# Splitting the first block's projections and summing the experts by token rows in a two-block fp32 model kernel

## The chip, the cores and the metric

The kernel runs on one core of a Trainium2 chip. Its engines are TensorE (PE: matmuls, and PEld: its weight loads), VectorE (DVE), ScalarE (ACT), GpSimd (POOL) and SyncE (SP, which only issues DMAs here). Each runs its own instruction list in order and waits on semaphores. The metric is the device time of one execution, in microseconds (us).

## The reference, cut to what matters

256 tokens of 1024 features (plus 16 meta tokens in the first block) go through two transformer blocks, all in float32:

```python
# first block
proj = rmsnorm(h) @ w_in                 # sb_q, sb_k, sb_v, df_q, df_k, df_v: 1024 columns each
o_sb = stick_breaking(sb_q, sb_k, sb_v)  # 8 heads
o_df = diff_attn(df_q, df_k, df_v)       # 8 heads
gates = sigmoid(xn @ w_gate + b_gate)    # 2048 columns
h = h + (gates[0] * (o_sb @ w_br_sb) + gates[1] * (o_df @ w_br_df)) @ w_out
h = h + (silu(hn @ w_ffn_gate) * (hn @ w_ffn_up)) @ w_ffn_down
x = rmsnorm(h)
# second block
mod = silu(c) @ w_ada + b_ada            # 6 x 1024: shifts, scales, gains gt_a and gt_f
...                                      # retention, dilated attention, projections
x = x + gt_f * moe(modulated norm of x)  # 32 experts, top 4 of each token
return rms_norm(x, g_final)
```

An expert takes the tokens routed to it through `u = x @ w1 + b1`, a clamped SwiGLU and `a @ w2 + b2`, and its result is added to the tokens' rows with their gate weights.

## The kernel before, in words

**Projections of the first block.** Activations lie feature by feature (`xn`: 8 tiles k of 128 features x 272 tokens). The weights come in 20 pieces of 1024 x 512 (`PIECES1`): sq, sk, sv twice, dq, dk, dv twice, four of gate, and two each of ysb, ydf and out. A piece makes four groups; the list of groups is `GR1`, and `G` steps in `ORDER1` are its groups. For the first 16 pieces a q, k or gate group is 8 plain float32 products of 256 or 272 columns (`group`, L1619), which the trace shows as two matmul records each. A v piece is a small group for the meta rows (L1602), two groups of 8 products with 512 columns, and one product that adds the meta rows up (L1608). The last six pieces are split: ScalarE rounds a quarter of a piece (128 x 1024 elements) to a high part (`high1`), VectorE subtracts it to get the low part (`low1`), and TensorE makes three products (high x high, high x low, low x high) in the fp32r type instead of one (`three`, L1629 to L1631). `high1` and `low1` run three groups ahead of the products.

**The attention heads lie between the groups.** `order1` gives every step a position: `G` g stands at position g, and a chain (start, period, heads, steps) puts step s of head h at start + period x h + offset. At one position head steps come before the group, later heads first. All engines walk through this one order, each doing its share of a step and skipping steps in which it has none. For the eight sb heads: `sbA` makes the scores (PE, L1672 to L1674), scales them (ACT), clips them (DVE), takes exp and ln (ACT) and finishes with three DVE operations, the last of them L1134; `sbB` multiplies by a triangle (PE, L1680 to L1685) and goes through DVE and ACT; `sbC` multiplies by the values (PE, L1694 to L1696). For the df heads there are `dfA` to `dfD`.

**Modulation.** The product with `w_ada` is made on VectorE: `modulation(j)` sums eight weighted rows of a 1024 x 512 piece of `w_ada` (L1088, then L1091 and L1093: eight operations, j = 0 to 11) into `adac`, and TensorE adds up the partitions in `ada_mm(j)` (L1663), which waits for that sum (`ada_sum`). `ada_mm` stands at the head of TensorE's part of `sbC` (j = h), and of `dfC` for the first four df heads (j = 8 + h).

**Experts.** Before them the router picks experts (DVE) and TensorE turns the tokens to rows (`htok`, L1932). For each expert TensorE gathers 64 tokens (L1986), makes `u` in four pieces (`up1`, L1976), `y` (L2013) and scatters the result back by `scatter` (L1960), which VectorE adds to `acc`. `acc` lies feature by feature; it starts as the bias term (L2033, eight products, copied by DVE at L1509) between expert 0 and expert 1. SP loads 12.6 MB of weights for an expert into six ring slots; piece c of the next expert's `w1` is loaded when `up1` has used that slot. After the last expert DVE adds `acc` times the gain to the residual (L1553), a norm follows (squares on ACT, L1564 on PE, root on ACT, L1048 on DVE), TensorE turns the result to token rows (L1932), ACT copies it, and one DMA stores 1 MB.

## Time and profile before

| | |
|---|---|
| median of 3 runs | 1971.28 us (1970.89 to 1972.0) |
| the profiled execution's own time | 1971.77 us |
| its span, first to last instruction | 1970.0 us |
| mean granted TensorE clock | 0.977 of 2.4 GHz |
| busy: PE, PEld | 1863.7 us, 1239.0 us |
| busy: DVE, ACT, POOL | 711.1 us, 554.3 us, 27.2 us |
| moved by DMA | 568.57 MB |

The profile is of one execution. Its span is 1.8 us less than its own time. "Busy" of PE counts overlapping matmuls, so it does not say at what rate they run; the spacing of starts does. PEclk is the granted clock, 1.00 for 2.4 GHz and 0.50 for 1.2 GHz.

### The profile page before, as it was taken

What the parts mean: (1) busy time and instruction counts of PE and PEld (TensorE: products, weight loads), DVE (VectorE), ACT (ScalarE), POOL (GpSimd) and SP (SyncE); (2) the same over time, 40 slices, a digit from 0 to 9 for tenths busy, and PEclk for the clock granted to TensorE, in tenths of its full rate; (3) what the DMA queues carried; (4) which work ended last, traced back from release to release, by engine and by line L of the source; (5) the groups of instructions that cost most, each with busy time, mean ns of one, the idle gap of its engine ahead of it and who ended that gap; (6) DMA issues with size and microseconds to landing.
All of it is one profiled execution on the core that took longest, in us unless ns stands there. A gap on an engine that the chain in (4) does not pass through costs nothing.

```text
span 1970.0 us, 26848 instructions
## 1 busy us (share of the span) xinstructions
PE 1863.7 (95%) x10951; PEld 1239.0 (63%) x10952; DVE 711.1 (36%) x1269; ACT 554.3 (28%) x916; POOL 27.2 (1%) x49
## 2 busy tenths in 40 slices
PE   7999989989998999999989999999999999999996
PEld 6666757989998799889853444344344344344343
DVE  2345533656654644546431222122122122122113
ACT  2344346544344455555410101001001000010002
POOL 2000000000000000000000000000000000000000
PEclk9999999999999999999879999999999999999997
DMA  7666423546554654534849999999999999999992
GB/s 245 221 215 214 171 86 129 171 134 195 184 206 135 201 179 150 170 109 166 315 177 378 428 430 428 429 428 429 428 429 428 429 428 429 428 429 428 429 428 111
DMA packets 135055, 568.57 MB, mean 289 GB/s; under 512 B 5552, under 2 KB 77336, under 8 KB 110288
## 3 DMA queue, kind: packets, MB, share of 16 engines
q1 hardware_dynamic: 127056, 536.60, 68.6%
q0 software_dynamic: 7936, 31.07, 4.5%
q8 instruction: 47, 0.77, 0.2%
q14 instruction: 16, 0.13, 0.0%
HBM read 566.58 MB, written 3.43 MB: 289 GB/s over the span
## 4 chain that ended last, share of the span: by engine, by line
PE 61%; DMA 33%; ACT 3%; DVE 2%; issue 1%; SPq 0%; DVEq 0%
DMA s_ring<-in_w_mlp 32%; PE banks L1619 11%; PE banks L1976 10%; PE banks L1629 6%; PE banks L1631 6%; PE banks L1630 6%; PE banks L1758 3%; PE banks L1759 3%; PE banks L1760 3%; PE banks L2013 3%; PE banks L1986 2%; PE banks L1564 1%; PE banks L1960 1%; PE banks L1663 1%; DVE s_W L1048 1%
## 5 line engine op out<-in xcount | busy, mean ns | idle before, releaser
L1976 PE MATMUL banks<-s_ring,s_W 128*64 128x512 f32 x2048 | 461.9, 599 | 29.1 <-DMA s_ring<-in_w_mlp 29.0
L1976 PEld LDWEIGHTS banks<-s_ring,s_W 128*64 128x64 f32 x2048 | 139.6, 137 | 319.1 <-issue 257.4
L1465 DVE TENSOR_TENSOR s_W<-banks,s_W 128x512 f32<-128x512 f32 x128 | 82.1, 683 | 633.7 <-PE banks L1960 633.7
L2013 PE MATMUL banks<-s_ring,s_W 128*64 128x512 f32 x1024 | 227.3, 597 | 0.3 <-ACT s_W L1000 0.3
L1619 PE MATMUL banks<-s_W,s_ring 128*128 128x256 f32 (+1 forms) x768 | 180.0, 391 | 4.6 <-DVE s_W L1048 4.6
L1619 PEld LDWEIGHTS banks<-s_W,s_ring 128*128 128x128 f32 x768 | 146.1, 193 | 33.6 <-issue 10.5
L2013 PEld LDWEIGHTS banks<-s_ring,s_W 128*64 128x64 f32 x1024 | 73.7, 138 | 148.2 <-issue 133.7
L1264 DVE TENSOR_TENSOR r_w2l<-s_ring,r_w2h 128x1024 fp32r<-128x1024 f32 x96 | 116.9, 1223 | 83.9 <-ACT r_w2h L865 83.7
L1005 ACT ACTIVATE s_W<-banks 128x512 f32<-128x512 f32 x32 | 19.1, 597 | 431.0 <-PE banks L2013 431.0
L1629 PE MATMUL banks<-r_x2h,r_w2h 128*128 128x256 f32 x448 | 130.7, 292 | 6.1 <-DVE r_x2l L1278 6.1
L1986 PEld LDWEIGHTS banks<-s_W 128*128 128x128 f32 x1024 | 123.2, 200 | 13.5 <-issue 11.4
L1986 PE MATMUL banks<-s_W 128*128 128x64 f32 x1024 | 127.7, 286 | 2.7 <-DVE s_W L1509 1.7
L1631 PE MATMUL banks<-r_x2h,r_w2l 128*128 128x256 f32 x448 | 127.4, 284 | 0.0
L1630 PE MATMUL banks<-r_x2l,r_w2h 128*128 128x256 f32 x448 | 127.3, 284 | 0.0
L865 ACT ACTIVATE r_w2h<-s_ring 128x1024 fp32r<-128x1024 f32 x96 | 100.8, 1053 | 46.2 <-PE banks L1631 36.3
L1009 ACT ACTIVATE s_W<-s_W 128x512 f32<-128x512 f32 x32 | 20.2, 631 | 325.4 <-DVE s_W L1483 325.4
L1758 PE MATMUL banks<-r_xfh,r_wh 128*128 128x256 f32 x352 | 100.4, 285 | 6.7 <-DVEq L1249 6.7
L1217 DVE TENSOR_TENSOR r_wl<-s_ring,r_wh 128x1024 fp32r<-128x1024 f32 x66 | 80.5, 1223 | 63.0 <-ACT r_wh L816 62.5
L1759 PE MATMUL banks<-r_xfl,r_wh 128*128 128x256 f32 x352 | 100.2, 285 | 0.0
L1760 PE MATMUL banks<-r_xfh,r_wl 128*128 128x256 f32 x352 | 100.1, 284 | 0.0
L1629 PEld LDWEIGHTS banks<-r_x2h,r_w2h 128*128 128x128 f32 x448 | 86.6, 193 | 7.6 <-issue 7.3
L1630 PEld LDWEIGHTS banks<-r_x2l,r_w2h 128*128 128x128 f32 x448 | 86.6, 193 | 0.5 <-issue 0.2
(382 smaller groups left out, 2770.0 us busy)
## 6 DMA issues: line engine op xcount, KB each, us to landing
s_ring<-in_w_mlp SPq DMA_DIRECT2D x192, 2048.0 KB, 22.4
s_ring<-in_w_in SPq DMA_DIRECT2D x38, 1024.0 KB, 5.0
s_ring<-in_w_in SPq DMA_DIRECT2D x12, 2048.0 KB, 9.1
...
```

Of the source, the lines that this page charges most:

```text
L865: act.activation(w2h[:, n % 4, :].rearrange("p (k n) -> p k n", k=raw.shape[1]), raw, ACT.Copy).then_inc(S["w_hi"], 1)
L1264: tt(unit2(w2l, n), raw, w2h[:, n % 4, :].bitcast(F32).rearrange("p (k n) -> p k n", k=raw.shape[1]), ALU.subtract).then_inc(S["w_lo"], 1)
L1619: last = mm(o, lhs, rhs, start=k == 0, stop=k == nk - 1)
L1629: mm(out, a[0], b[0], start=start, stop=False)
L1630: mm(out, a[0], b[1], start=False, stop=False)
L1631: return mm(out, a[1], b[0], start=False, stop=stop)
L1758: mm(out, wh[:, i, v], xh, start=start, stop=False, skip_group_check=True)
L1759: mm(out, wh[:, i, v], xl, start=False, stop=False, skip_group_check=True)
L1760: return mm(out, wl[:, i, v], xh, start=False, stop=stop, skip_group_check=True)
L1976: last = mm(pb[b][64 * h:64 * h + 64, :], XgT[:, 2 * c + k, :], slot(c, 2)[:, k, 1024 * h + 512 * b:1024 * h + 512 * b + 512], start=False ...
L1986: last = mm(pb[3][:, 64 * k:64 * k + 64], htok[:, t, P * k:P * k + P], selU[:, t, :], start=t == 0, stop=t == 1)
L2013: last = mm(pb[2][64 * h:64 * h + 64, :], aT[:, k, 64 * c:64 * c + 64], slot(4 + c, 4)[:, k, 512 * h:512 * h + 512], start=c == 0 and k == ...
```

## The change

Four things are changed.

1. The first 16 pieces are split like the last six. `xn` gets a high and a low part (`xnh`, `xnl`), and every q, k and gate group becomes 24 fp32r products. A v piece becomes four units of 18 products with 512 columns, over three row tiles (16 meta rows, 128 and 128 tokens), without the separate adding of meta rows. Positions of `ORDER1` are now units (`UNITS1`); pieces still have four. Weights come in halves of 1 MB throughout.
2. The heads start at unit 9 instead of group 12. `sbC` stands at offset 4 (was 3), `dfB` at 2.9 (2), `dfC` at 4 (3), `dfD` at 5 (4).
3. A modulation's eight operations are eight steps, `ada0` to `ada7`, three eighths of a unit apart, from unit 10 (it was one step at group 11, 14, ...).
4. `acc` lies by token rows and starts as residual plus bias term: TensorE makes rows of the gain (`spread`), turns the residual (`hx`) by products with the unit matrix, and adds the scaled bias term before expert 0. `yv` is multiplied by the gain on VectorE instead of copied on ScalarE. `scatter` has two products of 512 columns instead of four of 256. The final norm works by rows: two squares with a sum on ACT, two roots, two DVE operations, and a store for each half.

The gate and up products of the first block's feed-forward part are not touched.

```diff
-PIECES1 = ([(side + kind, n, i) for side in "sd" for i in range(2) for kind, n in (("q", 4), ("k", 4), ("v", 4))]
+PIECES1 = ([(side + kind, n, i) for side in "sd" for i in range(2) for kind, n in (("q", 4), ("k", 4), ("v", 3))]
...
 def order1():
-    return weave(len(GR1), (SB_AT, 3, HEADS, {"sbA": 0, "sbB": 2, "sbC": 3}),
-                 (SB_AT - 1, 3, ADAS, {"ada": 0}),
-                 (SB_AT + 3 * HEADS + 1, 3, HEADS, {"dfA": 0, "dfB": 2, "dfC": 3, "dfD": 4}),
...
+    return weave(len(UNITS1), (SB_AT, 3, HEADS, {"sbA": 0, "sbB": 2, "sbC": 4}),
+                 (SB_AT + 1, 3, ADAS, {f"ada{k}": 3 * k / KT for k in range(KT)}),
+                 (SB_AT + 3 * HEADS + 1, 3, HEADS, {"dfA": 0, "dfB": 2.9, "dfC": 4, "dfD": 5}),
...
-SB_AT = 12
+SB_AT = 9
...
         act.activation(vec[:, 0:NVEC], pb[5][:, 0:NVEC], ACT.Copy).then_inc(S["vec_kept"], 1)
+        for n in range(2):
+            high1(n)
         act.wait_ge(S["filled"], 1)
         root(0, rms, TM)
+        for t in range(KT):
+            act.wait_ge(S["norm_x"], t + 1)
+            act.activation(xnh[:, t, :], xn[:, t, :], ACT.Copy).then_inc(S["xn_hi"], 1)
+        high1(2)
...
+        for t in range(KT):
+            dve.wait_ge(S["xn_hi"], t + 1)
+            tt(xnl[:, t, :], xn[:, t, :], xnh[:, t, :].bitcast(F32), ALU.subtract).then_inc(S["xn_lo"], 1)
...
+            if k == 0:
+                if j >= 2:
+                    dve.wait_ge(S["ada_mm"], j - 1)
+                dve.wait_ge(S["csil"], 1)
+                dve.wait_ge(ina[b], 16 * (j // 2 + 1))
+                last = ts(adac[:, b, :], w[:, 0, :], csil[:, 0:1], None, ALU.mult)
+            else:
+                dve.wait_ge(S["ada_sum"], KT * j + k)
+                last = stt(adac[:, b, :], w[:, k, :], csil[:, k:k + 1], adac[:, b, :], ALU.mult, ALU.add)
+            last.then_inc(S["ada_sum"], 1)
...
         def ada_mm(j):
-            pe.wait_ge(S["ada_sum"], j + 1)
+            pe.wait_ge(S["ada_sum"], KT * (j + 1))
...
+        def spread(bank, cols, n):
+
+            for j in range(4):
+                c = cols[:, 4 * n + j:4 * n + j + 1].broadcast_to([P, P])
+                last = mm(pb[bank][:, P * j:P * j + P], c, ident, start=True, stop=True)
+            return last
...
-        for t in range(KT):
-            stt(hx[:, t, :], acc[:, t, :], modT[:, 40 + t:41 + t], hx[:, t, :], ALU.mult, ALU.add).then_inc(S["final_sum"], 1)
-        norm(5, hn, hx, nrms, vrows("g_final"))
+        dve.sem_inc(S["final_sum"], 1)
+        dve.wait_ge(S["spread_kept"], 6)
+        for t in range(2):
+            dve.wait_ge(S["fin_sq"], t + 1)
+            st.do(nc.vector.reciprocal(tr[:, t:t + 1], tr[:, t:t + 1]))
+            st.wait()
+            stt(otok[:, t, :], acc[:, t, :], tr[:, t:t + 1], gfb, ALU.mult, ALU.mult).then_inc(S["fin_kept"], 1)
```

What order each engine's instructions stand in, at three places. First VectorE, before: the eight operations of modulation 0 (L1088, L1091, L1093), then `sbA` of head 0 (L1127 to L1134).

```order
L1088 TENSOR_SCALAR s_W<-s_W,s_vx 128x512 [waits ada_in0,csil,cst_in]
L1091 SCALAR_TENSOR_TENSOR s_W<-s_W,s_vx 128x512 [waits dve_step] x6
L1093 SCALAR_TENSOR_TENSOR s_W<-s_W,s_vx 128x512 [waits dve_step]
L1127 TENSOR_SCALAR s_ring<-s_ring 128x384 [waits sb_zs]
L1128 TENSOR_SCALAR s_ring<-s_ring 16x256
L1131 TENSOR_TENSOR s_ring<-s_ring 128x384 [waits sb_ln]
L1132 TENSOR_TENSOR s_ring<-s_ring 16x256
L1134 TENSOR_TENSOR s_ring<-s_ring,s_cst 128x2x128 [waits dve_step]
```

VectorE now, at the `sbA` step of head 1 (L1157 to L1164): three steps of modulation 0 (L1122), the `sbA` step, the low part of a weight unit (L1084), the last two steps of modulation 0, and the first step of modulation 1 (L1119).

```order
L1122 SCALAR_TENSOR_TENSOR s_W<-s_W,s_vx 128x512 [waits ada_sum] x3
L1157 TENSOR_SCALAR s_ring<-s_ring 128x384 [waits sb_ln,sb_zs]
L1158 TENSOR_SCALAR s_ring<-s_ring 16x256
L1161 TENSOR_TENSOR s_ring<-s_ring 128x384 [waits sb_ln]
L1162 TENSOR_TENSOR s_ring<-s_ring 16x256
L1164 TENSOR_TENSOR s_ring<-s_ring,s_cst 128x2x128 [waits dve_step]
L1084 TENSOR_TENSOR r_w2l<-s_ring,r_w2h 128x8x128 [waits w1_hi]
L1122 SCALAR_TENSOR_TENSOR s_W<-s_W,s_vx 128x512 [waits ada_sum] x2
L1119 TENSOR_SCALAR s_W<-s_ring,s_vx 128x512 [waits ada_in1,csil]
```

Modulation 0 stood wholly ahead of `sbA` of head 0; now its last two steps stand behind `sbA` of head 1 and a weight unit. Modulations 1 to 6 stand likewise behind `sbA` of heads 2 to 7.

Second TensorE, before: `sbA` of head 1 (L1672 to L1674), `ada_mm(0)` (L1663) and `sbC` of head 0 (L1694 on), and the next group (L1619).

```order
L1672 MATMUL banks<-s_W 128x256 [waits sb_zs,act_evac1]
L1673 MATMUL banks<-s_W 128x128
L1674 MATMUL banks<-s_W 16x256
L1663 MATMUL banks<-s_ones,s_W 128x1 [waits ada_sum,act_evac1,sb_a]
L1663 MATMUL banks<-s_ones,s_W 128x1 x3
L1694 MATMUL banks<-s_ring,s_W 128x256
L1619 MATMUL banks<-s_W,s_ring 128x256 [waits act_evac1]
```

TensorE now, from `sbA` of head 1 (L1679 to L1681): unit 12 (24 products, L1626 to L1628), then `ada_mm(0)` (L1670) and `sbC` of head 0 (L1701), then the next unit.

```order
L1679 MATMUL banks<-s_W 128x256 [waits sb_zs,act_evac1]
L1680 MATMUL banks<-s_W 128x128
L1681 MATMUL banks<-s_W 16x256
L1626 MATMUL banks<-r_xnh,r_w2h 128x256 [waits act_evac1,w1_lo]
L1627 MATMUL banks<-r_xnl,r_w2h 128x256
L1628 MATMUL banks<-r_xnh,r_w2l 128x256
...
L1670 MATMUL banks<-s_ones,s_W 128x1 [waits ada_sum,act_evac1,sb_a]
L1670 MATMUL banks<-s_ones,s_W 128x1 x3
L1701 MATMUL banks<-s_ring,s_W 128x256
L1626 MATMUL banks<-r_xnh,r_w2h 128x256 [waits act_evac1,w1_lo]
```

One unit now stands between `sbA` of head h + 1 and `sbC` of head h, and `ada_mm` still waits for the modulation's last step.

Third TensorE ahead of the experts, before: tokens turned to rows (L1932), the router's ranks (L1943 on), the gate weights turned (L1949), gather of expert 0 (L1986), bias rows (L1967), `up1` (L1976), then the bias term (L2033) and the gather of expert 1 (rows that only repeat are left out).

```order
L1932 MATMUL banks<-s_cst,s_W 128x128 x16
L1943 MATMUL banks<-s_W,s_cst 128x32 [waits route]
L1949 MATMUL banks<-s_cst,s_W 32x128 x2
L1986 MATMUL banks<-s_W 128x64 [waits selu,rank_done,ht_kept]
L1967 MATMUL banks<-r_b1r,r_selB 128x512 [waits selb]
L1976 MATMUL banks<-s_ring,s_W 64x512 [waits expert_in0,xg]
L2033 MATMUL banks<-s_W 128x256 [waits gt_kept]
L1986 MATMUL banks<-s_W 128x64 [waits xg,selu,acc_init]
```

TensorE now: two `spread` of the gain (L1954), the residual turned (L1962), ranks (L1965), gate weights turned (L1972), the bias term (L1978), gather of expert 0 (L2012), `up1` (L2002), two `spread` of the final gain (L1954) and the gather of expert 1.

```order
L1939 MATMUL banks<-s_cst,s_W 128x128 x16
L1954 MATMUL banks<-s_cst,s_modT 128x128 x8
L1962 MATMUL banks<-s_cst,s_hT 128x128 [waits ht_kept]
L1965 MATMUL banks<-s_W,s_cst 128x32 [waits route]
L1972 MATMUL banks<-s_cst,s_W 32x128 [waits spread_kept]
L1978 MATMUL banks<-s_W 128x512 [waits b2_scaled,gt_kept]
L2012 MATMUL banks<-s_W 128x64 [waits selu,rank_done]
L1993 MATMUL banks<-r_b1r,r_selB 128x512 [waits selb]
L2002 MATMUL banks<-s_ring,s_W 64x512 [waits expert_in0,xg]
L1954 MATMUL banks<-s_cst,s_vec 128x128 [waits acc_init]
L2012 MATMUL banks<-s_W 128x64 [waits xg,selu]
```

The bias term has moved from behind expert 0 to ahead of its gather, and waits there for VectorE's scaled bias (`b2_scaled`).

## Rows read from the trace of the kernel before

**Rows 1.** the page's chain that ended last, by line, share of the span

```profile
DMA s_ring<-in_w_mlp 32%; PE banks L1619 11%; PE banks L1976 10%; PE banks L1629 6%; PE banks L1631 6%; PE banks L1630 6%; PE banks L1758 3%; PE banks L1759 3%; PE banks L1760 3%; PE banks L2013 3%; PE banks L1986 2%; PE banks L1564 1%; PE banks L1960 1%; PE banks L1663 1%; DVE s_W L1048 1%
```

**Rows 2.** stages: busy time by engine, granted clock, DMA share, GB/s

```profile
245.00:300.00 55.00, 50.01 (x217) 32.49 (x216) 19.68 (x50) 23.87 (x57) 0.00 (x0) 0.97 0.26 92
...
1200.00:1930.00 730.00, 700.11 (x3766) 307.78 (x3764) 151.95 (x320) 64.47 (x125) 0.00 (x0) 1.00 1.01 429
```

**Rows 3.** timeline and two lines' listings (ns min/median/max, first and last start), projections

```profile
53.17 1.92 PE L1602 MATMUL banks<-s_ring,s_W 128*32 128x512 f32 x16
69.92 0.48 PE L1672 MATMUL banks<-s_W 128*128 128x256 f32 x1
...
237.53 3.83 PE L1619 MATMUL banks<-s_W,s_ring 128*128 128x272 f32 x16
...
346.46 7.07 PE L1619 MATMUL banks<-s_W,s_ring 128*128 128x256 f32 x32
...
677.93 0.40 PE L1630 MATMUL banks<-r_w2l,r_x2h 128*128 128x512 f32 x1
...
689.53 0.39 PE L1630 MATMUL banks<-r_w2l,r_x2h 128*128 128x512 f32 x1
...
L1631 PE MATMUL banks<-r_dfh,r_w2l x64: 283/283/283, 376.6 to 399.3; 128*128 128x256 f32 x64
...
L1619 PE MATMUL banks<-s_W,s_ring x768: 379/379/634, 22.8 to 353.2; 128*128 128x256 f32 x128, 128*128 128x272 f32 x64
```

**Rows 4.** timeline and a window at the start of the projections

```profile
22.19 3.39 DVE L1048 SCALAR_TENSOR_TENSOR s_W<-s_hT,s_vec,s_ring 128x272 f32<-128x272 f32 x8 [8.10 <-ACT s_ring L678]
22.84 30.41 PE L1619 MATMUL banks<-s_W,s_ring 128*128 128x256 f32 x128 [4.64 <-DVE s_W L1048]
...
24.00:26.00 2.00, 2.00 (x6) 1.64 (x5) 1.97 (x6) 0.00 (x0) 0.00 (x0) 0.50 0.00 0
```

**Rows 5.** timeline around one sbA step (head 2): scores, chain, modulation

```profile
101.77 0.60 PE L1674 MATMUL banks<-s_W 128*16 128x256 f32 x2
102.30 1.05 PE L1663 MATMUL banks<-s_ones,s_W 128*128 128x1 f32 x8
...
107.87 0.42 DVE L1134 TENSOR_TENSOR s_ring<-s_ring,s_cst 128x256 f32<-128x256 f32 x1
...
108.73 4.69 DVE L1091 SCALAR_TENSOR_TENSOR s_W<-s_ring,s_vx,s_W 128x512 f32<-128x512 f32 x6
```

**Rows 6.** the page's groups: the split's two passes in the second block, mean ns

```profile
L1264 DVE TENSOR_TENSOR r_w2l<-s_ring,r_w2h 128x1024 fp32r<-128x1024 f32 x96 | 116.9, 1223 | 83.9 <-ACT r_w2h L865 83.7
...
L865 ACT ACTIVATE r_w2h<-s_ring 128x1024 fp32r<-128x1024 f32 x96 | 100.8, 1053 | 46.2 <-PE banks L1631 36.3
```

**Rows 7.** timeline: TensorE after a wait in the second kind of heads

```profile
274.82 0.30 PE L1719 MATMUL banks<-s_cst,s_ring 128*128 128x128 f32 x1 [2.90 <-ACT s_ring L762]
...
275.40 5.31 PE L1619 MATMUL banks<-s_W,s_ring 128*128 128x256 f32 x16
```

**Rows 8.** timeline and a window from routing to the second expert

```profile
995.07 7.06 PE L1986 MATMUL banks<-s_W 128*128 128x64 f32 x32 [0.99 <-DVE s_W L1452]
...
1003.02 15.70 PE L1976 MATMUL banks<-s_ring,s_W 128*64 128x512 f32 x64
1018.65 3.72 PE L2033 MATMUL banks<-s_W 32*128 32x256 f32 x16
...
1024.10 7.09 PE L1986 MATMUL banks<-s_W 128*128 128x64 f32 x32 [1.73 <-DVE s_W L1509]
...
1036.00:1038.00 2.00, 2.00 (x12) 0.67 (x10) 0.00 (x0) 0.00 (x0) 0.00 (x0) 1.00 0.00 0
...
1084.45 3.79 PE L1986 MATMUL banks<-s_W 128*128 128x64 f32 x32
```

**Rows 9.** timeline at the end of the program

```profile
1950.64 3.25 DVE L1553 SCALAR_TENSOR_TENSOR s_hT<-s_W,s_modT,s_hT 128x256 f32<-128x256 f32 x8 [1.58 <-issue]
...
1965.66 0.40 SPq L611 DMA_DIRECT2D out<-s_W  x1
```

More of the change, by code:

```diff
@@ L363, in program @@
     htok = area(W, 2048, 2, D)
[L364 removed]
+    acc = area(W, 4096, 2, D)
     selU = area(W, 6144, 2, 64)
@@ L985, in _ @@
                            ACT.Copy).then_inc(S["ht_kept"], 1)
+        for b in range(2):
+            act.wait_ge(S["spread"], b + 1)
+            act.activation(gtb[:, 512 * b:512 * b + 512], pb[3 - b], ACT.Copy).then_inc(S["spread_kept"], 1)
         act.wait_ge(S["route"], 1)
@@ L1011, in _ @@
         expert(0, True, False)
+        for b in range(2):
+            act.wait_ge(S["spread"], b + 3)
+            act.activation(gfb[:, 512 * b:512 * b + 512], pb[6 + b], ACT.Copy).then_inc(S["spread_kept"], 1)
         expert(1, True, True)
@@ new lines, in first_unit @@
+            if kind in V_KINDS:
+                groups = UNITS1[n // 4 * 4 + 3]
+                for kk in range(2):
+                    k = 2 * (n % 4) + kk
+                    for i, g in enumerate(groups):
+                        if k == 0:
+                            bank_free(GR1, g, both)
+                        v, rows = (slice(0, M), M) if i == 0 else (slice(M + P * (i - 1), M + P * i), P)
+                        last = three(pb[g % 3][0:rows, :], (xnh[:, k, v], xnl[:, k, v]), (whi[:, kk, :], wlo[:, kk, :]), k == 0, k == KT - 1)
+                        if k == KT - 1:
+                            last.then_inc(S["gemm1"], 1)
+                if n % 4 < 3:
+                    last.then_inc(S["v_unit1"], 1)
+                return
@@ new lines, in first_unit @@
+            xh, xl = {"ydf": (dfh, dfl), "ysb": (yh, yl), "out": (yh, yl)}.get(kind, (xnh, xnl))
+            tokens = slice(M, TM) if kind in ("sq", "dq", "gate") else slice(0, xh.shape[2])
+            for g in UNITS1[n]:
+                bank_free(GR1, g, both)
+                for k in range(KT):
+                    if n == 0:
+                        pe.wait_ge(S["xn_lo"], k + 1)
+                    if kind == "out":
+                        pe.wait_ge(S["y_lo"], 4 + k + 1)
+                    x = (xh[:, k, tokens], xl[:, k, tokens])
+                    last = three(pb[g % 3][:, 0:x[0].shape[1]], (whi[:, k, :], wlo[:, k, :]), x, k == 0, k == KT - 1)
+                last.then_inc(S["gemm1"], 1)
```

342 lines of the change are left out of this document (151 added, 191 removed).

## The prediction

> **What bounds the kernel now.** I read the page's chain first. Its largest link is the stream of expert weights (32% of the span), and most of the rest is TensorE, with L1619, the first block's products, at 11% [rows 1]. The windows agree: between 1200 and 1930 us the DMA engines are busy all the time (share 1.01, 429 GB/s), while in the first block, 245 to 300 us, TensorE works 50.0 of 55 us at DMA share 0.26 [rows 2]. So an instruction saved on TensorE, ACT or DVE per expert is worth nothing after 1200 us; what counts is the first block, the entry to the experts until the stream is the bound, and the tail. I read those at the spacing of starts, since busy time counts overlaps. The sum is made against the profiled execution's 1971.8 us (span 1970.0 and 1.8 around it), 0.5 above the median.
>
> **Projections on TensorE.** 32 records of 256 columns took 7.07 us; without the last record's 0.38, 31 spacings of 0.216 are left, so a q or gate group costs 3.45 us. A k group (272 columns, 3.83 for 16) costs 16 x 0.230 = 3.68. A v piece took from 53.17 to 69.92, 16.75 [rows 3]. The split products: 63 spacings from 376.6 to 399.3 us make one triple 0.360, so 24 products cost 2.88. With 272 columns the nearest row is that one times 272/256, 3.06 (bounds 2.88 and 3.45). For 512 columns, 677.93 to 689.53 is 17 triples, 0.227 a product, so the 72 products of a v piece cost 16.4 [rows 3]. Sum: 32 x 0.57 = -18.2, 16 x 0.62 = -9.9, 4 x 0.35 = -1.4: **-29.5**. The two passes for a weight unit, 1.05 us on ACT and 1.22 on DVE [rows 6], are shorter than a unit and lie beside it, so alone they add nothing.
>
> The Trainium skill ("FP8 and Floating Point Precision", TensorE Precision Notes) says that a true float32 product takes four passes; three passes for four would bring a group of 3.45 to 2.59 and this term to -42. The rows give 17% off, not 25%; I go by them.
>
> **Start.** Today the first product starts at 22.84, behind the first of eight multiplications that last 3.39 us together, and TensorE is at 0.50 of its clock then [rows 4]. Now two `high1` (2 x 1.05 [rows 6]) stand ahead of ACT's root, and then all eight low parts (about 0.45 each) stand on DVE behind all eight multiplications. First complete product: 22.84 + 2.1 + 3.4 less what overlaps, about 28. **+4.9** (bounds +2, the two passes alone, and +7, if the first two units' low parts hold the multiplications up as well).
>
> **A new wait at `sbC`.** This is the term that decides. `ada_mm(h)` opens TensorE's part of `sbC(h)` and waits for the eighth operation of modulation h. The order shows its last two operations behind `sbA(h + 1)` and one low part on VectorE; on TensorE a single unit lies between the same `sbA(h + 1)` and `ada_mm(h)`. Today the chain of an `sbA` runs on ACT and DVE in turn: scores end at 102.37, L1134 ends at 108.29, 5.9 us later, in which DVE is held by waits for ACT [rows 5]. Behind it come the low part 1.22 [rows 6], two operations of 0.78 [rows 5] and some 0.2 of signalling: ready 8.9 us after the scores. TensorE arrives after one unit, 2.9 (a v unit 4.1). Wait 6.0 for six heads and 4.8 for the one with a v unit, h = 0 to 6: **+40.8**. Queued behind the waiting `ada_mm` are `sbC(h)` and all later units; nothing overtakes. Head 7 has no `sbA` behind it and the df heads' `ada_mm` stands after `dfA`, whose DVE part is shorter. Lower bound of a wait: where TensorE arrives a unit later, 8.9 - 5.8 = 3.1; upper bound: 8.9, if it arrives at once.
>
> **The clock after such a wait.** At 274.82 TensorE had stood 2.90 us, and the next 16 records took 5.31 us where half of 7.07 is usual: +1.8. The opening groups show the same level, 0.50 at 24 to 26 us [rows 3, 4, 7]. Seven waits twice as long: 7 x 1.8 = **+12.6** (0, if a wait has no such price, to +18 with a longer slow stretch).
>
> The Trainium skill ("TensorE: Matmul & The Clock Gate", Part 1, on the clock gate) says that an idle TensorE falls back to half its clock and oscillates when gaps repeat; by this rule the 12.6 stands, and the trace's one row of 5.31 us agrees.
>
> **df heads and gates.** Today TensorE stands 5 of 55 us there and DVE works 19.7, which is 1.5 and 5.8 in a head of 16 us [rows 2]. On DVE a head now gains three low parts, 3.7 [rows 6], and the first four heads still have a modulation's eight operations, 6.2 [rows 5]: 15.7, about what TensorE needs, 16 - 1.5 - 3 x 0.57 = 12.8 and its waits. So up to 8 x 1.7 of the projections' saving can be lost to waits for DVE and ACT here; against that stand the wider steps of `dfB` to `dfD`. I take **+4** (0, all waits as before, to +8).
>
> Block 1: -29.5 + 4.9 + 40.8 + 12.6 + 4 = **+32.8**; the first block's other parts stay, so its first `ysb` product, behind the groups that end today at 346.46 + 7.07 [rows 3], starts near 386 instead of 353.
>
> **Entry to the experts.** The bias term costs 3.72 us now, and its copies 1.73 of waiting before the next gather, which also runs at half clock, 7.09 where the later one at 1084 us takes 3.79 [rows 8]. All of it leaves from behind expert 0: -5.45 and -3.3. In its place there comes the final gain's `spread`, half the columns: +1.9. Ahead of gather 0 come the bias term's products, as many columns as before (3.7, at half clock near 7), and ACT's copies and DVE's scaling of 1024 columns, 1.2 each; TensorE had been waiting 0.99 there for routing anyway, so part lies beside it. I take +4 (2 to 9). Net **-3** (-6.5 to +2). All of this counts in full, since the stream of weights stands still at 1036 us (DMA share 0.00) until `up1` of expert 1 frees a slot [rows 8]. In the steady part `scatter`, `yv` and their waits lie under the stream (share 1.01 [rows 2]): 0, and if that cover went, DVE's multiplication for ACT's copy would cost a few tenths of a us per expert.
>
> **Tail.** From L1553 at 1950.64 to the span's end is 19.4 us, 4.3 of it behind the store's issue at 1965.66 [rows 9]. In its place: two squares of 1024 columns on ACT (1.05 each by [rows 6]), a root and a reciprocal (0.2 each, my estimate from these rows' small operations), one multiplication of 1024 columns on DVE (1.5 by twice 0.78 [rows 5]) and a store of half the size (4): 8.1. **-11** (-9 to -12).
>
> **Sum:** 32.8 - 3 - 11 = +18.8, so 1990.6 against the profiled execution and **1990** against the median.
>
> **Rivals.**
> (a) *Faster: the modulation is done in time.* If DVE runs ahead of TensorE, so that the last two operations are ready when `ada_mm` comes up, the 40.8 and 12.6 vanish: 1971.3 - 29.5 + 4.9 + 4 - 3 - 11 = 1937 us. For that L1134's successor would have to end within half a microsecond of the scores; today's 5.9 speaks against it. The sign turns at a price per head (wait and clock) of (53.4 - 18.8) / 7 = 4.9 us, where I have 7.6. Chance 0.10, reaching to 1967.
> (b) *The waits come, but the clock does not fall:* 12.6 less, 1977 us. For it: the price rests on one row [rows 7]; against it: the waits are twice as long as the one there. Chance 0.14, from 1968 to 1982.
> (c) *DVE bounds all the df heads, and the entry stays at half clock:* +4 for the first, and +6 for the second (gather and bias term slow): 2000 us. For it: DVE's 15.7 a head; against: only four heads have modulations. Chance 0.17.
> (d) The sum as it stands, 1982 to 1996: chance 0.59.
>
> A measurement of this kernel tells about 0.2%, 4 us, from no change. Slower by more are (d), (c) and half of (b): 0.83. Within it 0.06, faster 0.11, from (b) and (a). The range leaves out (a) and the far end of (c): 1971 to 2003.
>
> **What the profile after would show.** TensorE idle some 6 us before `ada_mm` (L1670), released by DVE's L1122, seven times between 75 and 215 us, and a granted clock below 1 there; q units at 2.9 us; the first `ysb` product near 386 us; DMA share 1.0 between 1200 and 1930 still; some 8 us from the last addition to `acc` to the end. I am wrong if the waits at L1670 are under 4 us or bring no slow clock, if the last operation of an `sbA` (L1164 now) ends well before 5.9 us after its scores, or if the split products with 272 or 512 columns cost more than those of 256 per column.

## The result, and the profile after

The changed kernel takes 2018.99 us (median of 4 runs, 2016.09 to 2023.51); the kernel before, timed beside it, 1971.64 (1970.89 to 1972.42). The ratio is 1.0242, with a 95% interval of 1.022 to 1.0264: 47 us slower, where 19 were forecast (range up to 2003). The sign was right and the size was not. The profiled execution is the fastest of the four, with a span of 2014.5 us, 44.5 more than before.

The page's chain that ended last, by engine and by line, in the changed kernel:

```profile
PE 54%; DMA 33%; DVE 7%; ACT 5%; issue 2%; SPq 0%; DVEq 0%; ACTq 0%
DMA s_ring<-in_w_mlp 32%; PE banks L2002 9%; PE banks L1626 8%; PE banks L1628 7%; PE banks L1627 7%; PE banks L1765 3%; PE banks L1766 3%; PE banks L1767 3%; PE banks L2039 2%; DVE s_W L1122 2%; DVE r_w2l L1084 2%; PE banks L2012 1%; PE banks L1593 1%; ACT r_w2h L699 1%; PE banks L1670 1%
```

The stream of expert weights is still 32% of it [rows 1], but VectorE lines that were not there now are: L1122, a modulation step, and L1084, the low part of a weight unit. The list of waits (engine and line that waited, who released it, us in total, times, longest) names one for TensorE:

```profile
PE banks L1670 <- DVE s_W L1122: 45.7, 8, 7.2
```

These are eight waits of `ada_mm`, 45.7 us, the last of them 0.98 us; the seven before it make 44.7. One of them in full, around `sbA` of head 1 (timeline: start us, us, operation, idle before and its releaser):

```profile
75.95 0.61 PE L1681 MATMUL banks<-s_W 128*16 128x256 f32 x2
...
82.41 0.42 DVE L1164 TENSOR_TENSOR s_ring<-s_ring,s_cst 128x256 f32<-128x256 f32 x1
82.75 1.22 DVE L1084 TENSOR_TENSOR r_w2l<-s_ring,r_w2h 128x1024 fp32r<-128x1024 f32 x1
83.89 1.53 DVE L1122 SCALAR_TENSOR_TENSOR s_W<-s_W,s_vx 128x512 f32<-128x512 f32 x2
...
85.57 1.84 PE L1670 MATMUL banks<-s_ones,s_W 128*128 128x1 f32 x8 [5.98 <-DVE s_W L1122]
```

This is [rows 5] with the new things behind it: the scores end at 76.56, the chain 82.83, the low part and the last two modulation steps follow without a gap, and TensorE, after its single unit, has stood 5.98 us. The next row is what was not foreseen in its size. The windows of the same stretch (us, busy time of PE, PEld, DVE, ACT, POOL, granted clock, DMA share, GB/s), and after them those of the kernel before around its wait of 2.90 us [rows 7]:

```profile
79.00:82.00 3.00, 0.59 (x6) 0.39 (x4) 0.50 (x2) 2.97 (x5) 0.00 (x0) 1.00 0.27 94
82.00:83.50 1.50, 0.00 (x0) 0.00 (x0) 1.47 (x4) 0.67 (x2) 0.00 (x0) 0.57 0.00 0
85.00:95.00 10.00, 9.43 (x37) 8.40 (x38) 3.46 (x5) 1.33 (x2) 0.88 (x1) 0.50 0.60 210
95.00:97.00 2.00, 2.00 (x11) 1.46 (x9) 0.00 (x0) 1.48 (x2) 0.00 (x0) 0.78 0.19 25
```

```profile
275.00:276.00 1.00, 1.00 (x8) 0.91 (x7) 0.20 (x1) 0.56 (x3) 0.00 (x0) 1.00 1.04 406
276.00:279.00 3.00, 3.00 (x9) 2.36 (x9) 0.00 (x0) 0.34 (x2) 0.00 (x0) 0.52 1.04 395
279.00:280.00 1.00, 1.00 (x5) 0.86 (x4) 0.00 (x0) 0.00 (x0) 0.00 (x0) 0.73 0.08 27
280.00:282.00 2.00, 2.00 (x16) 1.28 (x15) 0.35 (x1) 0.48 (x1) 0.00 (x0) 1.00 0.00 0
```

The clock (1.00 is 2.4 GHz, 0.50 is 1.2) fell while TensorE idled and stayed at 0.50 through all of 85 to 95 us. Before, it fell after the wait had ended and was down for about 3.5 us. So `ada_mm`, `sbC` and most or all of a unit run at half speed in each of the seven heads (granted clock 0.50 to 0.59 from `ada_mm` to the next `sbB`), not only part of one group.

The kernel before has another row that bears on this. Behind its wait of 1.73 us ahead of the gather of expert 1 [rows 8] the clock was down for some 10 us, although the wait was shorter:

```profile
1022.00:1024.00 2.00, 0.37 (x2) 0.00 (x0) 2.00 (x4) 0.00 (x0) 0.00 (x0) 0.91 1.05 451
1024.00:1026.00 2.00, 1.91 (x9) 1.91 (x10) 0.64 (x3) 0.00 (x0) 0.00 (x0) 0.50 1.00 426
1032.00:1034.00 2.00, 2.00 (x7) 0.89 (x7) 0.00 (x0) 0.87 (x2) 0.00 (x0) 0.53 0.00 0
```

Ten microseconds at half speed are a price of about 5 us. Three other waits of that trace, 1.43, 1.81 and 2.05 us in the heads, cost nothing: the clock stayed at 1.00 behind them.

The stages one by one. The first product comes at 28.03 instead of 22.84 [rows 4]. The first block ends 57.3 us later (the first product behind its norm at 490.77, before at 433.50). The router's first product is at 1032.54, before at 974.99: the stretch between is the same within 0.3 us. From there to the third expert (the last row is cut off by the end of the view):

```profile
1055.33 7.19 PE L1978 MATMUL banks<-s_W 32*128 32x512 f32 x8 [0.46 <-ACT s_W L999]
1062.45 7.09 PE L2012 MATMUL banks<-s_W 128*128 128x64 f32 x32
1070.43 1.12 PE L2002 MATMUL banks<-s_ring,s_W 128*64 128x512 f32 x2
...
1087.00 3.68 PE L2012 MATMUL banks<-s_W 128*128 128x64 f32 x32
...
1114.77 1.44 PE L2012 MATMUL banks<-s_W 128*128 128x64 f32 x11
```

Gather 0 starts 29.9 us behind the router's first product (before 20.1 [rows 8]). Of these 9.8 us, 7.1 are the bias products, which ran at half clock, and 3.2 come before them: the ranks start 20.0 us behind the router's first product instead of 16.8, since VectorE now scales the bias rows first (1.21 us) and waits for ScalarE's copy of the gain until 1046.37. Behind gather 0 the time comes back: the gather of expert 1 takes 3.68 instead of 7.09, and from gather 0 to the third gather there are 52.3 us instead of 61.5. Up to the third gather the kernel is 0.7 us behind. The tail is 7.7 us from the first square to the span's end, and was 19.4 [rows 9]:

```profile
2006.77 1.06 ACT L1050 ACTIVATE s_W<-s_W 128x1024 f32<-128x1024 f32 x1 [12.65 <-DVEq L1577]
...
2009.86 1.74 SPq L616 DMA_DIRECT2D out<-s_W  x2
2009.94 1.28 DVE L1583 SCALAR_TENSOR_TENSOR s_W<-s_W,s_sml 128x1024 f32<-128x1024 f32 x1
```

Sum: 57.3 for the first block less 11.7 for the tail leaves 45.6 of the span's 44.5, so everything between gave back 1.1 and not 3. That is not from the entry either: what gave time back lies behind the third gather, 2.1 us, 1.1 of it in the last expert's `y` products, which took 8.10 us instead of 9.22 with less of them at half clock.

### The profile page after: what moved, and what is told of

It is laid out like the page before. It is cut to its first block, busy times and chain, and to the rows that moved or that the text cites. A ratio compares the mean times of both kernels' runs of the same rounds, so it can differ in the third digit from the quotient of the medians.

```text
span 2014.5 us, 27568 instructions
## 1 busy us (share of the span) xinstructions
PE 1858.4 (92%) x11191; PEld 1248.1 (62%) x11192; DVE 803.1 (40%) x1358; ACT 594.1 (29%) x952; POOL 27.1 (1%) x49
## 4 chain that ended last, share of the span: by engine, by line
PE 54%; DMA 33%; DVE 7%; ACT 5%; issue 2%; SPq 0%; DVEq 0%; ACTq 0%
DMA s_ring<-in_w_mlp 32%; PE banks L2002 9%; PE banks L1626 8%; PE banks L1628 7%; PE banks L1627 7%; PE banks L1765 3%; PE banks L1766 3%; PE banks L1767 3%; PE banks L2039 2%; DVE s_W L1122 2%; DVE r_w2l L1084 2%; PE banks L2012 1%; PE banks L1593 1%; ACT r_w2h L699 1%; PE banks L1670 1%
## 5 line engine op out<-in xcount | busy, mean ns | idle before, releaser
L2002 PE MATMUL banks<-s_ring,s_W 128*64 128x512 f32 x2048 | 460.6, 597 | 29.1 <-DMA s_ring<-in_w_mlp 29.1
L2002 PEld LDWEIGHTS banks<-s_ring,s_W 128*64 128x64 f32 x2048 | 139.1, 137 | 331.1 <-issue 258.6
L1501 DVE TENSOR_TENSOR s_W<-banks,s_W 128x512 f32<-128x512 f32 x32 | 22.1, 692 | 461.1 <-PE banks L2039 461.1
L1285 DVE TENSOR_TENSOR r_w2l<-s_ring,r_w2h 128x1024 fp32r<-128x1024 f32 x96 | 116.9, 1223 | 85.3 <-ACT r_w2h L872 85.0
L1084 DVE TENSOR_TENSOR r_w2l<-s_ring,r_w2h 128x1024 fp32r<-128x1024 f32 x88 | 107.3, 1223 | 91.2 <-ACT r_w2h L699 90.7
L1488 DVE TENSOR_TENSOR s_W<-banks,s_W 128x512 f32<-128x512 f32 x128 | 82.2, 684 | 147.5 <-PE banks L1987 147.5
L1626 PE MATMUL banks<-r_x2h,r_w2h 128*128 128x256 f32 x448 | 131.2, 293 | 6.1 <-DVE r_x2l L1299 6.1
L2012 PEld LDWEIGHTS banks<-s_W 128*128 128x128 f32 x1024 | 120.0, 196 | 24.2 <-issue 24.2
L1626 PE MATMUL banks<-r_xnh,r_w2h 128*128 128x256 f32 (+1 forms) x384 | 120.1, 313 | 9.7 <-DVE r_xnl L1092 9.7
L1628 PE MATMUL banks<-r_x2h,r_w2l 128*128 128x256 f32 x448 | 127.8, 285 | 0.0
L2012 PE MATMUL banks<-s_W 128*128 128x64 f32 x1024 | 124.3, 281 | 0.0
L1627 PE MATMUL banks<-r_xnl,r_w2h 128*128 128x256 f32 (+1 forms) x384 | 114.9, 299 | 0.0
L1628 PE MATMUL banks<-r_xnh,r_w2l 128*128 128x256 f32 (+1 forms) x384 | 114.8, 299 | 0.0
L872 ACT ACTIVATE r_w2h<-s_ring 128x1024 fp32r<-128x1024 f32 x96 | 100.8, 1053 | 46.1 <-PE banks L1628 39.7
L699 ACT ACTIVATE r_w2h<-s_ring 128x1024 fp32r<-128x1024 f32 x88 | 92.0, 1049 | 33.8 <-PE banks L1628 29.3
## 6 DMA issues: line engine op xcount, KB each, us to landing
s_ring<-in_w_mlp SPq DMA_DIRECT2D x192, 2048.0 KB, 22.4
```

What stands on the lines that cost most here:

```text
L699: act.activation(w2h[:, n % 4, :].rearrange("p (k n) -> p k n", k=raw.shape[1]), raw, ACT.Copy).then_inc(S["w1_hi"], 1)
L872: act.activation(w2h[:, n % 4, :].rearrange("p (k n) -> p k n", k=raw.shape[1]), raw, ACT.Copy).then_inc(S["w_hi"], 1)
L1084: tt(unit1(w2l, n), raw, w2h[:, n % 4, :].bitcast(F32).rearrange("p (k n) -> p k n", k=raw.shape[1]), ALU.subtract).then_inc(S["w1_lo"], 1)
L1285: tt(unit2(w2l, n), raw, w2h[:, n % 4, :].bitcast(F32).rearrange("p (k n) -> p k n", k=raw.shape[1]), ALU.subtract).then_inc(S["w_lo"], 1)
L1626: mm(out, a[0], b[0], start=start, stop=False)
L1627: mm(out, a[0], b[1], start=False, stop=False)
```

## The experiments

The theory, A: the modulation's last two operations stand on VectorE behind the next `sbA`, TensorE waits for them seven times, and each wait also costs the clock, some 4 us each and not 1.8. The price was worked out before the runs by adding the seven stretches from `ada_mm` to the next `sbB` (67.8 us in the changed kernel) against their length at full clock. The rivals: VectorE is simply overloaded; the clock is not the idling's doing; it is the new schedule as a whole that loses, so that the split under the old offsets would gain. The first four ran on one chip, the next four on another, the last four on a third; each ratio is against the kernel before on the same chip.

| run | base | median us | ratio (95%) |
|---|---|---|---|
| e_early | changed kernel | 1953.83 | 0.9911 (0.9894 to 0.9927) |
| e_whole | changed kernel | 1959.46 | 0.9940 (0.9924 to 0.9957) |
| e_fill | changed kernel | 1993.83 | 1.0115 (1.0098 to 1.0132) |
| e_sched | changed kernel | 1966.26 | 0.9984 (0.9974 to 0.9994) |
| e_half | kernel before | 1959.68 | 0.9942 (0.9928 to 0.9955) |
| e_start | e_early | 1948.70 | 0.9876 (0.9861 to 0.9891) |
| e_moe | e_early | 1953.31 | 0.9904 (0.9889 to 0.9920) |
| e_all | e_early | 1950.81 | 0.9892 (0.9877 to 0.9907) |
| e_c5 | changed kernel | 1994.23 | 1.0110 (1.0091 to 1.0130) |
| e_ada2 | e_start | 1949.40 | 0.9891 (0.9875 to 0.9906) |
| e_warm | e_start | 1946.95 | 0.9867 (0.9852 to 0.9882) |
| e_best | e_start | 1941.48 | 0.9855 (0.9839 to 0.9871) |

**e_early: one number.**

```diff
-                 (SB_AT + 1, 3, ADAS, {f"ada{k}": 3 * k / KT for k in range(KT)}),
+                 (SB_AT, 3, ADAS, {f"ada{k}": 3 * k / KT for k in range(KT)}),
```

> The changed kernel with one number altered: the eight modulation steps start one unit earlier, so that the last two stand ahead of sbA(h + 1) on VectorE and not behind it. Theory A (the wait at ada_mm is made by that place): the seven waits, 44.7 us together, and the half clock after them, some 28.6 us worked out from the changed kernel's trace, vanish: 2019 - 73 = 1946 us, between 1942 and 1956 with new small waits. Rival B (VectorE is overloaded in the sb heads or the sb chain itself is late, wherever the steps stand): the waits stay at another instruction, 1990 us or more. Rival C (waits go, the half clock stays because of other pauses): about 1974.

1953.8 us: 65 of the expected 73 came back, and the kernel is faster than before by 0.9%. VectorE does the same work, so the overload (B) is out. The windows from 75 to 250 us of this kernel and of the changed one:

```profile
75.00:250.00 175.00, 169.19 (x1026) 136.86 (x1026) 127.45 (x212) 100.78 (x181) 8.84 (x10) 0.95 0.62 217
```

```profile
75.00:250.00 175.00, 130.33 (x647) 104.91 (x645) 79.75 (x127) 67.48 (x112) 6.18 (x7) 0.77 0.41 137
```

Between the same times VectorE was busy 127 us instead of 80 and still had time; the clock rose from 0.77 to 0.95. A head without a wait runs as follows, 5.18 us from `ada_mm` to the next `sbB`, where the changed kernel needs 9.7:

```profile
84.21 0.95 PE L1670 MATMUL banks<-s_ones,s_W 128*128 128x1 f32 x8
...
89.39 0.39 PE L1687 MATMUL banks<-s_ring,s_cst 128*128 128x128 f32 x2
```

What is left are two waits, of 1.81 and 0.98 us. Both took the clock with them again, the first for some 10 us. The view of the first, and the windows from `ada_mm` to the next `sbB` behind each:

```profile
97.89 1.23 DVE L1084 TENSOR_TENSOR r_w2l<-s_ring,r_w2h 128x1024 fp32r<-128x1024 f32 x1 [1.85 <-ACT r_w2h L699]
99.03 1.53 DVE L1122 SCALAR_TENSOR_TENSOR s_W<-s_ring,s_vx,s_W 128x512 f32<-128x512 f32 x2
...
100.71 1.75 PE L1670 MATMUL banks<-s_ones,s_W 128*128 128x1 f32 x8 [1.81 <-DVE s_W L1122]
```

```profile
100.70:110.70 10.00, 9.99 (x39) 8.95 (x40) 6.67 (x12) 5.55 (x9) 0.88 (x1) 0.51 0.81 308
170.70:179.10 8.40, 8.40 (x39) 7.58 (x40) 5.11 (x10) 5.55 (x9) 0.88 (x1) 0.61 0.98 355
```

The seven stretches from `ada_mm` to `sbB` add up to 45.9 us here, 67.8 in the changed kernel and 38.4 at full clock. So the clock gave back 21.9, the waits 45.7 - 2.8 = 42.9, together 64.8 of the 65 measured; the missing 8 are the clock behind two short waits.

The split itself has gained little so far. Of the 17 us against the kernel before, 13 belong to the experts' part and the tail (e_half, below). From its first product to the one behind the norm the first block takes 402.6 us, before 410.7: 8 less, where the split's products alone should give 28. Longer waits of TensorE in it, 18.1 us against 9.4, took 9 of the rest; what remains, some 12 us, goes with the lower clock (0.95 over the block, before 0.99). And the first product came later (30.05, before 22.84).

**e_whole: the modulation in one piece again, at its old place.**

```diff
-                 (SB_AT + 1, 3, ADAS, {f"ada{k}": 3 * k / KT for k in range(KT)}),
+                 (SB_AT - 1, 3, ADAS, {f"ada{k}": k / 1000 for k in range(KT)}),
```

> The changed kernel, but all eight modulation steps stand together one unit ahead of sbA(h), where the kernel before had them. Theory A (place, not the cut into steps): like the run with earlier steps, 1946 us. Rival B: eight operations in one piece, 6.2 us, hold up the next sbA's VectorE part and with it sbB two units later, at 2.9 us a unit: some 2 to 3 us a head, about 1965. If the cut itself cost, it would be below 1946 by more than 4.

1959.5: the waits at `ada_mm` are gone here too, so the place made them and not the cut. But now `sbB` waits in six of eight heads, for the `sbA` part that stands behind the block of eight:

```profile
106.85 0.79 PE L1687 MATMUL banks<-s_ring,s_cst 128*128 128x128 f32 x2 [2.39 <-DVE s_ring L1164]
```

These waits are 0.9 to 2.4 us. By the medians the kernel is 5.6 us slower than single steps at a good place on the same chip; the two intervals just overlap. So the cut did not cost; whether it helps by itself is not shown, since the two kernels differ in the place of the steps too.

**e_fill: TensorE busy in the wait, nothing else changed.**

```diff
+                for _ in range(14 if h < 7 else 0):
+                    mm(pb[7][:, 0:T], sv[:, 0, v], la[:, 0:T], start=True, stop=True)
                 ada_mm(h)
```

> The changed kernel, in which TensorE makes 14 extra products of sbC's own operands (256 columns, about 0.43 us each, 6.0 us, overwritten by the real first product) ahead of each of the seven ada_mm that wait. The VectorE order and the lateness are as in the changed kernel. Theory A (idling is what brings the half clock, and it costs 28.6 us in all): the wait is filled, the clock stays 1.00, and the time falls to about 1990, 1986 to 1998. Rival B (the half clock comes from somewhere else, or the 28.6 is not its price): no gain, 2015 to 2022, or slower by the extra work where it outlasts the wait.

1993.8: 25 us came back although no modulation was ready earlier. The extra products could only fill the wait and keep the clock up:

```profile
75.00:250.00 175.00, 170.55 (x958) 138.03 (x956) 92.63 (x145) 76.18 (x125) 7.06 (x8) 0.97 0.46 156
```

The clock is 0.97 instead of 0.77 in the same stretch, and the seven stretches behind `ada_mm` take 43.5 us instead of 67.8, 24.3 less. So the clock's price in the changed kernel is 25 us by experiment and 29 by its trace; 12.6 were forecast. The remaining 40 (1993.8 to 1953.8) are in the main the waits themselves, 44.7 us by the trace.

**e_c5: `sbC` a unit later.**

```diff
-    return weave(len(UNITS1), (SB_AT, 3, HEADS, {"sbA": 0, "sbB": 2, "sbC": 4}),
+    return weave(len(UNITS1), (SB_AT, 3, HEADS, {"sbA": 0, "sbB": 2, "sbC": 4.9}),
```

> The changed kernel with sbC at offset 4.9 instead of 4, the modulation's place untouched: TensorE reaches ada_mm one unit, 2.9 us, later. Theory A (the modulation is ready at a fixed time after sbA's scores, so a wait is that time less the units between): each of the seven waits, 6.4 on average, shrinks to 3.5 us, -20 in all, and the half clock's price lies between 1.8 and 4.1 a head: 1983 to 2000 us, 1995 likeliest. Rival B (each wait is tied to something that moves with sbC): no change, 2015 to 2022. Rival C (3.5 us of idling no longer costs the clock): 2019 - 20 - 29 = 1970.

1994.2, as the arithmetic of a fixed ready time gives. Two of the waits at `ada_mm`:

```profile
86.54 1.02 PE L1670 MATMUL banks<-s_ones,s_W 128*128 128x1 f32 x8 [3.14 <-DVE s_W L1122]
...
132.67 1.84 PE L1670 MATMUL banks<-s_ones,s_W 128*128 128x1 f32 x8 [2.42 <-DVE s_W L1122]
```

There are six such waits, 3.14, 2.63, 2.42, 3.14, 2.59 and 2.41, 16.3 us in place of 44.7, and the one with the 512-column piece has shrunk to 0.24. Yet a wait of 2.42 still ends in half clock (the eight `ada_mm` records last 1.84 us, where 1.02 is the full clock's), and the granted clock from 75 to 250 us is 0.78, where the changed kernel has 0.77:

```profile
75.00:250.00 175.00, 158.44 (x757) 120.04 (x756) 93.49 (x150) 76.41 (x131) 7.06 (x8) 0.78 0.47 160
```

The 28 us less of waiting gave 25: shortening the waits gave none of the clock's price back.

**e_sched: the split projections under the old schedule.** `SB_AT = 12`, `sbC` at 3, `dfB` to `dfD` at 2, 3, 4, the modulation in one piece.

> The changed kernel's split projections, start, experts and tail, with the schedule of before: sb heads from unit 12, sbC at 3, dfB, dfC, dfD at 2, 3, 4, the modulation in one piece one unit ahead of sbA. Theory A (the loss is all in the new schedule, the split itself gains 29.5 and the start loses 5.2): block 1 ends some 20 to 24 us before that of the kernel before, and with -13 at the experts and the tail the time is 1936 to 1942. Rival B (shorter units leave the chains too little time at the old offsets): waits at sbB, sbC, dfB of 1 to 3 us each, 1950 to 1975.

1966.3: rival B. The split's gain is lost in new places; the longest of these waits are in the df heads:

```profile
240.61 0.70 PE L1747 MATMUL banks<-s_ring,s_ones 128*128 128x256 f32 x2 [3.62 <-ACT s_ring L775]
...
258.61 1.01 PE L1747 MATMUL banks<-s_ring,s_ones 128*128 128x256 f32 x2 [2.71 <-ACT s_ring L775]
```

`sbB` waits 0.6 to 2.4 us in six heads, much as in e_whole. Between e_sched and e_whole lie 7 us, which the earlier start of the heads and the wider offsets are worth together. A unit is 17% shorter than a group was (2.88 us for 3.45), so a chain's steps need more units between them. The new offsets were not the mistake, the modulation's place was.

**e_half: the experts' part and the tail alone, on the kernel before.** All of part 4 of the change, the first block untouched.

> The kernel before with the fourth part of the change alone: acc by token rows, spread, bias term ahead of expert 0, and the new tail. By the two traces the tail is 11.6 us shorter and the stage from the router to the end of the stream 1 to 3 us shorter: -13, about 1958 us (1955 to 1961). Rival: the stream of weights takes the entry's part back, or gives more, independent of the first block: only the tail's 11.6 counts, 1960, or with the bias term at half clock in the way (+10 at gather 0) and no gain behind, 1965 or more.

1959.7 against 1972.7: -13.0, as read from the two traces. Of the whole change's 47.4 us the first block thus cost 60 (57.3 in the profiled execution, which is 2.9 below the median).

**e_start: the first high and low parts ahead of the wait for the turned vector.**

```diff
+        for n in range(2):
+            high1(n)
         act.wait_ge(S["x_turned"], 6)
         act.activation(vec[:, 0:NVEC], pb[5][:, 0:NVEC], ACT.Copy).then_inc(S["vec_kept"], 1)
-        for n in range(2):
-            high1(n)
         act.wait_ge(S["filled"], 1)
```

and likewise `low1` on VectorE ahead of its wait for `vec_kept`.

> The kernel with earlier modulation steps, in which ACT makes the first two high parts ahead of its wait for the turned vector and VectorE their low parts ahead of its wait for it, so that the norm's root no longer stands behind them. In the changed kernel ACT stood idle 3.4 us there. Theory: the root comes 2 us earlier, the first product too: 2 us less than the kernel with earlier steps, 1952 us. Rival: the weights of the first unit land later than the idle time, then the wait for them holds the vector and the root: 0, or slower by 1 to 2.

1948.7. ACT does the two parts at 15.12 in time that was idle, and the table load for the root starts right behind the vector's copy:

```profile
15.12 1.99 ACT L697 ACTIVATE r_w2h<-s_ring 128x1024 fp32r<-128x1024 f32 x2
20.24 0.27 ACT L702 ACTIVATE s_vec<-banks 128x121 f32<-128x121 f32 x1 [3.13 <-PE banks L1616]
20.53 1.28 ACT L681 ACT_TABLE_LOAD   x1
```

It is 4.6 below e_moe on the same chip, and e_moe's own edit was worth nothing; 2 were expected. The traces say what the edit itself is worth: TensorE stands 7.9 us before the first product in every run that has it (e_start, e_all, e_ada2, e_warm, e_best) and 9.7 in every run of the changed kernel without it, so 1.8 us. The rest of the 4.6 is not explained by it. The first product also moves by about 2 us between runs of the same code (the changed kernel 28.03, e_early 30.05), because the 16 products of the first norm's sum (L1593) took 3.91 us in one and 6.36 in the other.

**e_moe: the bias products back behind expert 0, the final gain's `spread` ahead of the ranks.**

```diff
+        expert(0, True, False)
+        pe.wait_ge(S["gt_kept"], 1)
+        pe.wait_ge(S["b2_scaled"], 1)
+        for b in range(4):
+            t, half = b // 2, b % 2
+            mm(pb[4 + b], gatT[:, P * t:P * t + P], b2s[:, 512 * half:512 * half + 512], start=False, stop=True, skip_group_check=True)\
...
```

> The kernel with earlier modulation steps, in which the four bias products go back behind expert 0, and the final gain's spread comes forward into TensorE's wait for routing. The products took 7.2 us at half clock ahead of gather 0; behind expert 0 they should take 3.7 at the full clock, where the spread's 2.05 leaves: 7.2 - 3.7 + 2.0 = 5.5 less, plus a pause for ACT's four copies at half a us: -4 to -5.5 against the kernel with earlier steps, 1949 us. Rival: the stream bounds from expert 0 on, and nothing moves: 1954.

1953.3, no gain against e_early's 0.9911: the expectation failed. The products took 3.69 as thought, and gather 0 came 22.7 us behind the router's first product instead of 27.9 in e_early. But the gather behind them fell back to 7.09:

```profile
1015.90 3.69 PE L2060 MATMUL banks<-s_W 32*128 32x512 f32 x8
...
1020.29 7.09 PE L2011 MATMUL banks<-s_W 128*128 128x64 f32 x32 [0.69 <-ACT s_W L1029]
```

```profile
1018.00:1020.00 2.00, 1.60 (x4) 0.37 (x2) 0.80 (x2) 1.80 (x4) 0.00 (x0) 1.00 1.11 475
1020.00:1024.00 4.00, 3.71 (x18) 3.71 (x18) 0.60 (x2) 0.23 (x1) 0.00 (x0) 0.54 0.97 414
```

Ahead of gather 0, 5.1 us were won. Behind expert 0, 4.4 came back for the products and the pause for their copies, 3.4 for the gather (7.09 for 3.68), and 2.05 left with the spread: +5.7. The kernel before has the same pair, 3.72 and 7.09 [rows 8]. So what the change won at gather 1 was the clock, and it hangs on what stands in front of it.

**e_all: e_start and e_moe together.**

> Earlier modulation steps, the reordered start and the moved bias products together. If the two gains add: 1954 - 2 - 5 = 1947 us (1944 to 1950). If either was lost to a wait elsewhere, 1949 to 1954.

1950.8, 2.1 above e_start on the same chip: e_moe's edit had nothing to add.

**e_ada2: the steps another 0.4 unit earlier**, `SB_AT - 0.4` in the line of e_early, with e_start's order.

> The kernel with the reordered start, and the modulation steps another 0.4 unit earlier, so that the last stands 0.8 units ahead of sbA(h + 1). Theory: the two to four waits of 1 to 1.8 us at ada_mm that are left, and the half clock after the first of them (5.6 us for a unit of 3.1), go: -4 to -7 us, 1943 us. Rival: those waits are for the modulation's own data or for VectorE's load as a whole, and stay: 1949.

1949.4, where 1943 were expected and e_start had 1948.7 on another chip: no gain is shown by this pair. On one chip e_best and e_warm differ by exactly this edit, and e_best is 5.5 us faster. But not all of that is the edit's: in the profiled executions, which differ by 8.4, the first block is only 2.1 us shorter (395.3 for 397.3); the first product came 2.0 earlier and the entry to the experts ran 2.8 faster, at more of the full clock, and the edit touches neither. The largest wait at `ada_mm` is 0.96 instead of 1.77; waits of 1 us stay, whose cause was not looked for.

**e_warm: extra products in two waits ahead of the experts.** 16 products that nobody reads.

```diff
         norm(4, nsq, T, SQUARED)
+        for _ in range(9):
+            mm(pb[1][:, 0:T], ones[:, :], nsq[:, 0, :], start=True, stop=True)
...
+        pe.wait_ge(S["route"], 1)
+        for _ in range(7):
+            mm(pb[1][:, 0:T], ones[:, :], nsq[:, 0, :], start=True, stop=True)
         pe.wait_ge(S["route"], 2)
```

> The kernel with the reordered start and the earlier steps, in which TensorE makes 16 extra products that nobody reads, 9 in its wait for the last norm ahead of the router and 7 in its wait for routing. In the changed kernel the router's products (7.0 us), the bias products (7.2) and gather 0 (7.1) all ran at half clock behind these two waits. Theory (idling costs the clock there too): each halves nearly, -9 to -11 us, 1938 us. Rival: the clock comes back late whatever is done, or the extra products delay the router: 1948 to 1953.

1946.95, where 1938 were expected. Its base e_start ran on another chip (1948.7), 1.8 us above. On the same chip the edit stands between e_ada2 and e_best, 1949.4 and 1941.5, which is 7.9 us of the 9 to 11 expected. From the router's first product to gather 0 there are 25.2 us (e_start 29.9, e_best 22.4): in e_warm the router's products still took 6.8 us and the bias products 4.9. What else is missing is in the next trace.

**e_best: e_start, e_ada2 and e_warm.**

> Reordered start, modulation steps 0.4 unit earlier and the two filled waits together. If the gains add: 1949 - 5 - 10 = 1934 us (1931 to 1939). If the filled waits bring nothing, 1943; if neither does, 1949.

1941.5, ratio 0.9855: 1934 were expected if the gains add, and the range of 1931 to 1939 was missed by 2.5. It is the fastest kernel here, 30 us below the kernel before on its chip and some 77 below the changed one. The entry to the experts in it:

```profile
962.83 4.89 PE L1947 MATMUL banks<-s_W 128*128 128x32 f32 x32
...
981.62 3.70 PE L1982 MATMUL banks<-s_W 32*128 32x512 f32 x8 [0.46 <-ACT s_W L999]
985.24 7.03 PE L2016 MATMUL banks<-s_W 128*128 128x64 f32 x32
```

```profile
983.00:985.00 2.00, 2.00 (x6) 0.74 (x4) 1.95 (x3) 1.48 (x3) 0.00 (x0) 1.00 0.00 0
985.00:986.00 1.00, 1.00 (x5) 0.76 (x5) 0.01 (x1) 0.69 (x2) 0.00 (x0) 0.67 0.00 0
986.00:987.00 1.00, 1.00 (x7) 1.00 (x6) 0.00 (x0) 0.00 (x0) 0.00 (x0) 0.50 0.00 0
```

The router's 32 products take 4.9 us instead of 7.0 and the bias products 3.70 instead of 7.2: here the filled waits did their work. Then the clock falls between 985 and 986 us with TensorE busy all through, and the gather takes 7.03 anyway.

## Why the prediction was wrong

Its mechanism was right, and the term "the clock after such a wait" was mis-sized.

- **Projections, -29.5: right.** The changed kernel's units repeat at 2.9 us (256 columns), 3.13 (272) and 4.17 for a v unit. The 3.06 for 272 columns was 0.07 short, 1.1 us in all, so -28.4. The quarter less that three passes for four would give did not come, as the rows had said. (The -42 named for it counts the q, k and gate groups alone.)
- **Start, +4.9: right**, 5.2 measured (28.03 for 22.84).
- **The wait at `sbC`, +40.8: right in place and number**, 44.7 measured, and 1.0 more in an eighth wait that was not foreseen. The 5.98 of head 0 is the 6.0 worked out. The others were 7.17, 6.80, 4.75, 5.95, 7.22 and 6.80. At head 1 the low part and three modulation steps (2.32 us) still ran on VectorE when `sbA`'s scores were done, so the chain itself began late; this and the like make up the missing 4 us.
- **The clock, +12.6: the step that failed.** The prediction took 1.8 us per wait from one row, at a wait of 2.90 us [rows 7], multiplied it by seven and gave "0 to 18" as bounds. The seven stretches measure 67.8 us against 38.4 at full clock, 29.4 us or 4.2 a wait; e_fill gives 25 by experiment. In that one row the clock fell only after the wait had ended, and was down for 3.5 us; in the changed kernel it fell during the wait and was down for 7 to 10 us of work behind it. The length of the wait is no measure of this price. Behind 1.81 us it was 4.5 us in e_early and behind 1.76 at the same place 1.6 in e_moe, and in e_c5 six waits of 2.4 to 3.1 us left the clock as low as waits of 4.75 to 7.2 had (0.78 and 0.77). The kernel before could have warned of it: its wait of 1.73 us cost about 5 us, of which the prediction booked 3.3 at the entry to the experts [rows 8] without using the row here. So the upper bound, not only the value, was taken from the wrong row. The Trainium skill ("TensorE: Matmul & The Clock Gate", Part 1, HAM oscillation) tells of a clock that falls in every gap of a loop; the changed kernel's 0.77 over seven heads, where the kernel before has 1.00, agrees, and its size had to come from rows.
- **df heads, +4: right.** TensorE's waits there add up to 11.5 us (0.4 to 1.4 in seven places and 3.97 before the last `dfB`), before to 7.9: +3.6. **Left out** was a wait for banks (the buffers that products are written to): a v piece's first unit writes to three at once, and stood 1.87 us in one sb and 1.84 in one df piece, 3.7.
- **The first block added up:** 5.2 + 44.7 + 1.0 + 29.4 + 3.6 + 3.7 - 28.4, less 1.4 for a wait in the sb heads that the kernel before had and this one has not, make 57.8 of the 57.3 measured.
- **Entry to the experts, -3:** +0.7 up to the third gather. Gather 0 came 9.8 us later, beyond the "2 to 9"; behind it 9.2 us came back, where 6.9 were forecast, since after the gather of expert 1 some products run at full clock too that did not before. (The lower bound of -6.5 does not follow from the terms given: with 2 us ahead of gather 0 they make -4.9.)
- **Tail, -11: right**, -11.7.
- **The rivals.** (a) is the kernel with the modulation in time: it said 1937, and e_early shows 1954. It had set the clock's price at 0 once the long waits were gone, while e_early still lost some 12 us to it in the first block and 5 more than foreseen to waits. (b) was wrong; (c)'s half clock at the entry came true.

The range's upper end, 2003, was exceeded by 16 us, about what the clock's term was short: 29.4 in place of 12.6.
